# A two-layer hybrid trunk step on one core: mixing's multiply and subtract on VectorE, matmul filler held back for the attentions' ends, sink diagonals on ScalarE, first norm shared out

## The reference

```python
h = layer_norm(x) * (1 + scale) + shift            # adaLN from c (latent) or c_ctx (context)
p = h @ w_in                                        # 4096 columns: qa ka va ga qb kb vb gb uc vc gc
A: 8 q heads / 2 kv heads, d = 64, rms-normed q and k, axial rotary; full attention; context keys cached
B: same heads, windowed |i-j| <= 128, a learned sink logit per head in the softmax's denominator
C: per chunk of 128 positions and per group of 128 channels:
   y = u * (w_mix[g] @ v_n + b_mix[g])              # full 128x128 mixing over positions
each branch: o = out * silu(gate), y_r = o @ w_out_r
merge = sum over r of sigmoid(h @ w_gate_r) * y_r   # per-channel merge gates
x = layer_norm(ALPHA * x + gate_adaLN * (merge @ w_out), ln_g, ln_b)
```

## Time and profile before

| | |
|---|---|
| median of 3 runs | 1574.95 us (1574.42 to 1575.47) |
| the profiled execution's own time | 1575.67 us |
| its span | 1573.9 us |
| TensorE (matmul) busy | 1463.9 us, 93% |
| VectorE busy | 818.6 us, 52% |
| GpSimd busy | 796.3 us, 51% |
| ScalarE busy | 556.6 us, 35% |
| data moved | 126.90 MB, 81 GB/s over the span |

### The profile page before, as it was taken

The page is one execution under the profiler, slowest core; times in us unless marked ns, Lnnn a source line. Parts: engine busy times, 40 slices in busy tenths (PEclk is TensorE's granted clock), DMA queues, the critical chain, the costliest instruction groups (busy, mean ns, idle before and its releaser), DMA issues.

```text
span 1573.9 us, 21752 instructions
## 1 busy us (share of the span) xinstructions
PE 1463.9 (93%) x8776; PEld 1322.8 (84%) x8776; DVE 818.6 (52%) x1237; ACT 556.6 (35%) x843; POOL 796.3 (51%) x565
## 2 busy tenths in 40 slices
PE   4998998999998999899989999988999989998996
PEld 3798887889887888899868988887988879997985
DVE  4675677461788421111784757764448774011147
ACT  2333554333653211203233345542356422221130
POOL 1444676333666433724674547743246654464354
PEclk9999999999999999999999999999999999999999
DMA  7412000121100343344320220012111012214231
GB/s 301 144 54 71 27 28 14 67 71 67 41 28 27 117 151 123 132 147 146 122 86 35 85 67 28 27 41 71 54 54 41 27 47 101 81 68 166 89 107 67
DMA packets 36612, 126.90 MB, mean 81 GB/s; under 512 B 5024, under 2 KB 5664, under 8 KB 36512
## 3 DMA queue, kind: packets, MB, share of 16 engines
q1 hardware_dynamic: 29808, 108.54, 19.9%
q10 hardware_dynamic: 6704, 16.97, 2.9%
HBM read 119.73 MB, written 5.77 MB: 80 GB/s over the span
## 4 chain that ended last, share of the span: by engine, by line
PE 79%; DVE 9%; POOL 6%; issue 2%; ACT 2%; DVEq 0%; POOLq 0%; ACTq 0%
PE ps L899 43%; PE ps L847 6%; PE ps L849 6%; PE ps L848 6%; PE ps L1031 2%; PE ps L1029 2%; PE ps L1081 2%; PE ps L1058 2%; PE ps L1078 2%; POOL w_lo L1725 2%; PE ps L1057 2%; DVE o_inv L1610 2%; PE ps L1079 2%; PE ps L916 1%; POOL o_lo L1770 1%
## 5 line engine op out<-in xcount | busy, mean ns | idle before, releaser
L1725 POOL TENSOR_TENSOR w_lo<-raw,w_hi 128x1024 fp32r<-128x1024 f32 x148 | 359.2, 2434 | 345.0 <-ACT w_hi L1124 344.7
L899 PE MATMUL ps<-h_hi,w_hi 128*128 128x320 f32 x1280 | 300.0, 316 | 12.8 <-DVE g_c L1622 6.4
L899 PE MATMUL ps<-h_lo,w_hi 128*128 128x320 f32 x1280 | 293.6, 311 | 0.0
L899 PE MATMUL ps<-h_hi,w_lo 128*128 128x320 f32 x1280 | 293.3, 310 | 0.0
L1753 POOL TENSOR_TENSOR p_lo<-p_f,p_hi 128x512 fp32r<-128x512 f32 x164 | 212.7, 1301 | 155.1 <-ACT p_hi L1267 154.9
L899 PEld LDWEIGHTS ps<-h_hi,w_hi 128*128 128x128 f32 x1280 | 218.7, 190 | 34.0 <-DVE g_c L1622 8.1
L899 PEld LDWEIGHTS ps<-h_lo,w_hi 128*128 128x128 f32 x1280 | 217.1, 190 | 2.4
L899 PEld LDWEIGHTS ps<-h_hi,w_lo 128*128 128x128 f32 x1280 | 216.2, 189 | 2.4
L1124 ACT ACTIVATE w_hi<-raw 128x1024 fp32r<-128x1024 f32 x148 | 152.8, 1050 | 85.4 <-DMA raw<-in_weights 42.0
L1637 DVE TENSOR_TENSOR gy<-ps,sg 128x640 f32<-128x640 f32 x32 | 26.4, 824 | 255.5 <-PE ps L899 255.4
L1558 DVE TENSOR_REDUCE top<-ps 128x1 f32<-128x512 f32 (+1 forms) x128 | 83.5, 656 | 125.9 <-PE ps L1036 86.9
(11 more groups left out here) (177 smaller groups left out, 2640.4 us busy)
## 6 DMA issues: line engine op xcount, KB each, us to landing
raw<-in_weights SPq DMA_DIRECT2D x190, 512.0 KB, 3.3
raw_more<-in_weights SPq DMA_DIRECT2D x10, 512.0 KB, 10.7
x<-in_x_sample ACTq DMA_DIRECT2D x6, 512.0 KB, 8.0
x_mid<-x ACTq DMA_DIRECT2D x5, 512.0 KB, 2.6
x<-x_mid ACTq DMA_DIRECT2D x5, 512.0 KB, 6.7
y_sample<-x SPq DMA_DIRECT2D x4, 512.0 KB, 2.6
pack<-in_pack ACTq DMA_DIRECT2D x2, 528.0 KB, 4.6
x<-in_x_sample SPq DMA_DIRECT2D x2, 512.0 KB, 4.9
```

The source lines that it names most:

```text
L899: last = pe.matmul(ps[:, s + half, 0:HALF], w[:, u % RING, cols], acts[:, k, half * HALF:(half + 1) * HALF], start=k == 0 and part == 0, s ...
L1725: did(pool.tensor_tensor(w_lo[:, n % RING, :], raw_tile(r), w_hi[:, n % RING, :], ALU.subtract), w_ready)
```

## The change

It has six parts.

1. Mixing's multiply and subtract go from GpSimd to VectorE, directly behind the add, and signal a semaphore of their own, `mixed`, on which the y of branch 2 waits. The order is now mix 0, mix 1, z 0, mix 2, mix 3, z 1, instead of mix 0, z 0, mix 1, mix 2, z 1, mix 3.
2. `attention` takes `last_filler`, which it puts ahead of the product of the last group's first step: the last 5 of 48 chunks in A, the last 3 of 48 in B. The others are spread as before.
3. The event `dg` is gone; ScalarE makes the four diagonals itself, in its rounding step of the SINK slot.
4. xn of tiles 0 to 2 is made by ScalarE (scale and bias from GpSimd's `nmr`), of tiles 3 and 4 by VectorE. The `mod_row` copies of the first layer go from VectorE to ScalarE. The second pair's mod events stand ahead of h. TensorE waits once for all five xn.
5. `ones` moves from ahead of the first query tiles to behind kv tile 2, and kv tiles 0 and 1 stand ahead of gate 2 of A.
6. The last tile's second half is added on VectorE; its last pass goes in two halves of 512 columns, each stored by a DMA of its own.

The diff, cut to its core:

```diff
@@ -144,8 +145,6 @@
 for n, (g, i) in enumerate(steps):
-    if group_slots(br, g)[i] == SINK:
-        out.append(("dg", l, br, g))
     out.append(("ST", l, br, g, i))
@@ -154,6 +153,8 @@
 tick()
+if n == first[count - 1]:
+    out.extend(last_filler)
 product(n)
@@ -177,13 +178,16 @@
 def mods(p):
-    pair = (p, KT_D // 2 + p)
-    out.extend(("mod", 0, b, half) for b in pair for half in range(2))
-    out.extend(("col", 0, b) for b in pair)
+    out.extend(("mod", 0, b, half) for b in (p, KT_D // 2 + p) for half in range(2))
+def cols(p):
+    out.extend(("col", 0, b) for b in (p, KT_D // 2 + p))
 mods(0)
+cols(0)
 out.append(("split", 0))
 out.extend(("ht", 0, j) for j in range(KT_D))
+mods(1)
 for p in range(KT_D // 2):
@@ -191,7 +195,9 @@
 if p + 1 < KT_D // 2:
-    mods(p + 1)
+    if p:
+        mods(p + 1)
+    cols(p + 1)
 out.append(("mm", 0, "q_a", p))
@@ -233,8 +239,6 @@
     out.append(("table", l))
-if l == 0:
-    out.append(("ones", l))
@@ -252,8 +256,8 @@
 out.extend([qs[1], qs[2], *whole(gate("a", 0)), queries[1], qs[3], *whole(gate("a", 1)), queries[2], qs[4],
-            kvm[0], queries[3], qs[0], kvm[1], queries[4], *whole(gate("a", 2)), queries[0], *kv[0:3],
-            *whole(gate("a", 3)), keys[0], kv[3], keys[1], kv[4], keys[2], *whole(("z", l, 0, 0)), keys[3], keys[5],
+            kvm[0], queries[3], qs[0], kvm[1], queries[4], kv[0], kv[1], *whole(gate("a", 2)), queries[0], kv[2],
+            ("ones", l), *whole(gate("a", 3)), keys[0], kv[3], keys[1], kv[4], keys[2], *whole(("z", l, 0, 0)), keys[3], keys[5],
             keys[4], *whole(("z", l, 0, 1))])
@@ -267,7 +271,7 @@
     filler[-1] = (filler[-1], ("z", l, 0, j))
-out.extend(flat(attention(l, "a", filler, 3, 2, 4)))
+out.extend(flat(attention(l, "a", filler[:-5], filler[-5:], 3, 2, 4)))
 out.append(("pool", 0, 1, 2, 3, 4, 5, 6, 7))
@@ -291,7 +295,7 @@
         filler[-1] = (filler[-1], gate(br, c))
-out.extend(flat(attention(l, "b", filler, 3, 2, 4)))
+out.extend(flat(attention(l, "b", filler[:-3], filler[-3:], 3, 2, 4)))
 out.append(("pool", 0, 1, 2, 3, 4, 5, 6, 7))
@@ -307,8 +311,8 @@
 if begun:
-    out.extend([("mix", l, 0), *whole(("z", l, r, 0)), ("mix", l, 1), ("mix", l, 2), *whole(("z", l, r, 1)),
-                ("mix", l, 3)])
+    out.extend([("mix", l, 0), ("mix", l, 1), *whole(("z", l, r, 0)), ("mix", l, 2), ("mix", l, 3),
+                *whole(("z", l, r, 1))])
 else:
@@ -828,10 +832,17 @@
 for t in range(T):
-    sp.wait_ge(x_done, T * last + t + 1)
+    if t < T - 1:
+        sp.wait_ge(x_done, T * last + t + 1)
     dst = outs["y_prompt"][0] if t == 0 else outs["y_sample"][0, (t - 1) * P:t * P, :]
-    sp.dma_start(dst, x[:, t, :]).then_inc(final, 16)
-sp.wait_ge(final, 16 * T)
+    if t < T - 1:
+        sp.dma_start(dst, x[:, t, :]).then_inc(final, 16)
+    else:
+        for half in range(2):
+            sp.wait_ge(x_done, T * last + t + 1 + half)
+            cols = slice(half * BW, (half + 1) * BW)
+            sp.dma_start(dst[:, cols], x[:, t, cols]).then_inc(final, 16)
+sp.wait_ge(final, 16 * (T + 1))
@@ -974,8 +985,8 @@
 for t in range(T):
-    if j == 0:
-        pe.wait_ge(xn_ready, T * l + t + 1)
+    if j == 0 and t == 0:
+        pe.wait_ge(xn_ready, T)
     last = pe.transpose(slot(s)[:, t * P:(t + 1) * P], xn[:, t, j * P:(j + 1) * P], ident)
@@ -983,7 +994,10 @@
 if stage[0] == "y" and i == 0 and stage[3] == 0:
-    pe.wait_ge(o_done, O_PER_LAYER * l + (10, 20, 24)[stage[2]])
+    if stage[2] == 2:
+        pe.wait_ge(mixed, KT_B * (l + 1))
+    else:
+        pe.wait_ge(o_done, O_PER_LAYER * l + (10, 20)[stage[2]])
 channel_rows(stage, i, n)
@@ -1164,6 +1178,18 @@
     load(pack_loaded, pack[:, :], a["pack"][l])
+elif kind == "ln" and e[1] == 0:
+    for i, t in enumerate(XN_ON_ACT):
+        act.wait_ge(nmr_ready, i + 1)
+        did(act.activation(xn[:, t, :], x[:, t, :], ACT.Identity, bias=nmr[:, t:t + 1], scale=rstd[:, t:t + 1]),
+            xn_ready)
+elif kind == "mod" and e[1] == 0 and e[2] in FIRST_MODS:
+    if e[3]:
+        s = wait_filled(act, e[:3])
+        n = MODS.index(e[:3])
+        if n >= 2:
+            wait_filled(act, MOD_USER[n - 2])
+        did(act.activation(mod_row[:, n % 2, :], ps[:, s, 0:COLS], ACT.Copy), drained[s])
 elif kind == "h":
@@ -1259,7 +1285,12 @@
 if group_slots(br, g)[i] == SINK:
-    act.wait_ge(dg_made, NO[("dg",) + e[1:4]] + 1)
+    c = NO[("es",) + e[1:4]]
+    act.wait_ge(es_made, c + 1)
+    for h in range(GRP):
+        last = act.activation(p_f[:, n % 3, h * P:(h + 1) * P], ident, ACT.Copy, scale=es_f[:, c % 3, h:h + 1])
+        did(last, dg_made if h == GRP - 1 else None)
+    act.wait_ge(dg_made, c + 1)
 else:
@@ -1435,7 +1466,7 @@
 await_rstd()
-for t in range(T):
+for t in [t for t in range(T) if t not in XN_ON_ACT]:
     did(dve.tensor_scalar(xn[:, t, :], x[:, t, :], mv[:, t, 0:1], rstd[:, t:t + 1],
@@ -1454,7 +1485,7 @@
 elif kind == "mod":
-    if e[3] == 0:
+    if e[3] == 0 or e[1] == 0 and e[2] in FIRST_MODS:
         continue
@@ -1584,14 +1615,6 @@
                                  ALU.mult, ALU.mult), drained[s])
-elif kind == "dg":
-    step = ("ST",) + e[1:] + (len(group_slots(*e[2:])) - 1,)
-    n, c = NO[step], NO[("es",) + e[1:]] % 3
-    dve.wait_ge(es_made, NO[("es",) + e[1:]] + 1)
-    dve.wait_ge(p_lo_made, n - 2)
-    for h in range(GRP):
-        last = dve.tensor_scalar(p_f[:, n % 3, h * P:(h + 1) * P], ident, es_f[:, c, h:h + 1], None, ALU.mult)
-        did(last, dg_made if h == GRP - 1 else None)
 elif kind == "O":
@@ -1641,10 +1664,15 @@
     if n >= 2:
-        dve.wait_ge(o_done, O_DONE[MIXES[n - 2]])
+        dve.wait_ge(mixed, n - 1)
     did(dve.tensor_tensor(c_out[:, g % 2, :].rearrange("p (t n) -> p t n", t=T),
                           slot(s)[:, 0:TOK].rearrange("p (t n) -> p t n", t=T),
                           b_sp[:, g:g + 1, :].to_broadcast([P, T, P]), ALU.add), drained[s])
+    wait_drained(dve, ("gT", l, "u", g))
+    wait_drained(dve, e)
+    did(dve.tensor_tensor(c_out[:, g % 2, :], c_out[:, g % 2, :], g_c[:, g, :], ALU.mult), gated)
+    dve.wait_ge(o_hi_made, O_MADE[e])
+    did(dve.tensor_tensor(o_lo[:, g, :], c_out[:, g % 2, :], o_hi[:, g, :], ALU.subtract), mixed)
 elif kind == "m":
@@ -1662,6 +1690,10 @@
     drained[s])
+if (l, half, t) == (DEPTH - 1, 1, T - 1):
+    wait_drained(dve, e)
+    dve.wait_ge(x_alpha, T * l + t + 1)
+    half_summed[t] = did(dve.tensor_tensor(x[:, t, cols], x[:, t, cols], scaled[:, t % 2, :], ALU.add))
 if half == 0:
@@ -1669,7 +1701,8 @@
 after(half_summed[t])
-dve.wait_ge(x_summed, T * l + t + 1)
+if (l, t) != (DEPTH - 1, T - 1):
+    dve.wait_ge(x_summed, T * l + t + 1)
 ask_rstd(moments(t, [x[:, t, 0:512], x[:, t, 512:D]]))
@@ -1679,8 +1712,9 @@
     dve.wait_ge(ln_b_loaded, 16 * (l + 1))
-    did(dve.scalar_tensor_tensor(x[:, t, :], x[:, t, :], rstd[:, t:t + 1], ln_b_bc[:, :],
-                                 ALU.mult, ALU.add), x_done)
+    for cols in ((slice(0, BW), slice(BW, D)) if (l, t) == (DEPTH - 1, T - 1) else (slice(0, D),)):
+        did(dve.scalar_tensor_tensor(x[:, t, cols], x[:, t, cols], rstd[:, t:t + 1], ln_b_bc[:, cols],
+                                     ALU.mult, ALU.add), x_done)
 elif kind == "xt":
@@ -1732,12 +1771,12 @@
     root(rstd[:, t:t + 1], mv[:, t, 1:2], EPS, t)
-    pool.wait_ge(rstd_ready, asked[0])
-    pool.wait_ge(*did(pool.tensor_tensor(nmr[:, t:t + 1], mv[:, t, 0:1], rstd[:, t:t + 1], ALU.mult)))
-    did(pool.tensor_scalar(nmr[:, t:t + 1], nmr[:, t:t + 1], -1.0, None, ALU.mult), nmr_ready)
+    shift(t)
 elif kind == "ln" and e[1] == 0:
     for t in ARRIVAL:
         root(rstd[:, t:t + 1], mv[:, t, 1:2], EPS, t)
+        if t in XN_ON_ACT:
+            shift(t)
 elif kind in ("ln", "vn"):
@@ -1760,14 +1799,8 @@
     n = NO[e]
-    pool.wait_ge(o_hi_made, O_DONE[e])
+    pool.wait_ge(o_hi_made, O_MADE[e])
     did(pool.tensor_tensor(og_part(o_lo, g), og_sum(n), og_part(o_hi, g), ALU.subtract), o_done)
-elif kind == "mix":
-    _, l, g = e
-    wait_drained(pool, e)
-    did(pool.tensor_tensor(c_out[:, g % 2, :], c_out[:, g % 2, :], g_c[:, g, :], ALU.mult), gated)
-    pool.wait_ge(o_hi_made, O_DONE[e])
-    did(pool.tensor_tensor(o_lo[:, g, :], c_out[:, g % 2, :], o_hi[:, g, :], ALU.subtract), o_done)
 elif kind == "y" and e[2] >= 1:
@@ -1777,7 +1810,7 @@
     did(pool.tensor_tensor(kept_lo[n][:, :], raw_tile(r), kept_hi[n][:, :], ALU.subtract), kept)
-elif kind == "out" and e[2] == 1:
+elif kind == "out" and e[2] == 1 and e[1:] != (DEPTH - 1, 1, T - 1):
     _, l, _, t = e
```

27 lines of the change are left out of this document (16 added, 11 removed).

## The result

The changed kernel takes **1520.29 us** (median of 4 runs, 1520.01 to 1520.94) against 1574.68 of the kernel before in 4 runs (1573.22 to 1575.47). The ratio is 0.9657, 95% interval 0.964 to 0.9673: 54.4 us faster. The prediction said 1517, between 1504 and 1541. The profiled execution took 1520.94 us, its span is 1519.1, 54.8 shorter than before.

A forecast was written before the change was run, and what follows sets the result against it. TensorE was taken as the bound, busy 1463.9 of 1573.9 us, leaving only its idle time and lower-clock time to win. Terms summed to -58.5 from 1575.67, giving 1517 us, range 1504 to 1541.

The forecast's parts named there:

- One hold per layer: Mixing: a VectorE SBUF instruction waits beside a GpSimd w_lo pass, 2.1 us more; 1.5 us given back over both layers.
- the rival in which GpSimd holds VectorE through the stage: Mixing: its waits stay, +15 to 1532 us; chance 0.22, shared with the other 1532 case.
- 2.0 for the body: Attention bodies, thinner filler: one new wait of 1.0 us in each of four bodies, +4.0 us in all.
- The clock term: Behind the o_sum wait at attention A's end: slower clock loses 2.5 us per layer, counted as saved with the wait.
- 2.5 was taken: Attention B, diagonals on ScalarE: its own half of the g_c evictions gets later, 2.5 us given back.
- the 5.3: First norm: with three xn tiles and the mod_row copy on ScalarE, VectorE is through 5.3 us earlier, at about 19.8.
- The signs it named: Profile after, several stages: what waits, clock, VectorE times, ScalarE load and transposes' start should show if the forecast holds.
- the prediction's bound of 50 us: TensorE's list of waits: the forecast is wrong if they still add up to more than 50 us.
- ScalarE late in attention B: Rival, attention B: ScalarE's diagonals delay TensorE at each of 20 sink steps, 64 us, 1581 us; chance 0.05.
- The rival of the end chain that moves with the filler: Attentions' ends: o_sum moves back with TensorE, 27 us lost, 1544 us; chance 0.08, shared with both 1532 cases together.
- With nothing held up anywhere: Rival, whole kernel: no new waits anywhere, -75.9 us to 1500; chance 0.15 for 1500 to 1508.

The follow-up runs named there:

- The six-chunk run: The changed kernel with the last 6 chunks of attention B's filler held back for its end instead of 3; 1506.85 us.
- the best kernel here: The changed kernel with 6 chunks of attention B's filler held back and xn of tiles 0 to 3 on ScalarE; 1505.21 us.

## Why the prediction was right, and where it wasn't

**The total** is right by 3 us, and the signs of all six parts are. One size isn't, that of attention B with the diagonals, which came 8 us short. That the total is so close is in part luck: 3.7 us came in stretches that the sum didn't count and 1.1 more at mixing than was forecast.

**Part 1** (-15.0): 16.1 in the timeline. One hold per layer, as taken; the rival in which GpSimd holds VectorE through the stage stays away because GpSimd, now free, goes through both w_lo passes at once and is idle behind them (5.78 us ahead of 638.23), so only one of the four SBUF instructions of the last two groups meets it.
The Trainium skill, "GPSIMD Engine Reference", section 1, names VectorE instructions with two SBUF inputs as those that contend with GpSimd. The trace agrees with it on the multiply (2.07 and 2.33 instead of 0.82). The scaling of xn has one tensor input and is held just the same (3.56 us for two tiles, 0.81 for one alone). The section's other case, a two-port performance mode, would cover it. The rows fit that: a scaling takes 0.54 us for 512 elements and 0.81 for 1024, 0.5 ns for each more, while the multiply or subtract of two tensors takes 0.69 for 512 and 0.82 for 640, 1.0 ns for each more. No run here switches the mode off, so it isn't shown as the cause.

**Part 2, A** (-12.0 and 2.0 for the body): 9.7 in the timeline, 8.4 by undoing it. The waits were right to the hundredth, and the body cost 0 instead of 2. The clock term, 2.5 us in each layer, has to be looked for outside of the 9.7, because most of it lay behind the attention's end, in the kv_b stretch. Before, the five us behind this wait are at 0.50 in both layers (267.30 and 1034.80), now they are at 1.00. TensorE's idle time in the kv_b stretch is 5.26 us in both layers of both kernels, and its busy time fell by 0.1 us in layer 0 and by 3.0 in layer 1: this is where the row of 0.1 + 3.0 comes from. In layer 0 the gain was lost again behind the later wait of 2.99 us, where the clock was 1.00 before and is 0.66 now; in layer 1 it was 0.50 there and is 0.66. So the term was right where it was read, and wrong was to take the clock behind a wait as a loss that nothing else changes.

**Part 2, B, and part 3** (-15.0 and -5.5, 2.0 for the body; 18.5 in all): 7.9 us inside the attention, 10.7 with the v_c stage behind it, and 10.5 by undoing both. This is the step that was wrong, though the total held. The prediction had "one new wait of 1.0 us" for the thinner body; the profile has 4.12 and 3.48, and 4.0 more for ScalarE's g_c where 2.5 was taken. The rows for it were there before: the earlier trace rows list g_c with 6.4 us in 4, and the prediction took that for VectorE's load alone, which part 3 would relieve; it rose to 8.0. It is also the place of the chunk behind a gate's boundary, which needs the only pair of banks. The six-chunk run shows it: the same work on every engine, the chunks placed otherwise, and 13.4 us come out; of the waits that went, half were on VectorE's evictions and half on ScalarE's. And the two parts were added where they share a limit: undone singly they cost 1.4 and 2.6, together 10.5.

**Part 4** (-6.5): 6.4. The terms inside were off and cancelled: the transposes came 3.7 earlier (21.63 from 25.35) and not 5.3, because of the hold beside w_lo. (The prediction's words give the 5.3 to VectorE; by its own rows VectorE would be through at 19.8 instead of 17.51 + 5.73 = 23.24, 3.4 earlier, and 5.3 is what the transposes' start at "near 20" would gain.) Between them and the first q_a matmul another 2.7 came, where the second mod_row wait (3.1) went and a wait of 1.4 for h_lo took its place. Of the 6.4, 5.5 are idle time and 1.0 clock, which the sum hadn't counted there.

**Part 5** (-8.0): 7.3 in the timeline, 6.1 by undoing it. **Part 6** (-0.5): 0.8; the affine pass of the last tile but one is at 1.28 us from the 2.16 of the earlier trace rows.

**The signs it named.** No wait on mixing's low half, no o_sum wait, a clock of 1.00 behind both attentions and 82 us of ScalarE came as said; the transposes begin at 21.6 instead of near 20, and 1.9 us of k_st wait stayed. The seven lines of the earlier trace rows make up 55.8 us and not 53.8, and 11.7 now; the prediction's bound of 50 us can only be meant for them, since the whole list of waits is at 61.5.

**The rivals.** ScalarE late in attention B: it is busy 81.97 of 130.8 us there, the 82 that were worked out, and it cost waits of 4 us in all, not 64. The rival of the end chain that moves with the filler is refuted for A, and near the truth for B as long as the diagonals are on ScalarE, where 2.6 us is left of what the three chunks were to bring; with the diagonals on VectorE it is 9.1. With nothing held up anywhere the prediction had 1500; the best kernel here reaches 1505.

**Left open.** What decides whether a wait of a given length is followed by lost clock isn't shown, so the parts' clock losses can't be told from each other to better than 1 to 2 us. How much of the 13.4 us of the six-chunk run belongs to the moved chunk and how much to the new spacing wasn't separated. The memsets themselves weren't made smaller, and filler with a second pair of banks in B wasn't tried.

## What to carry to other kernels

Independent work that fills a wait has to be checked for what it waits for itself: with one buffer, the place of the piece that crosses from one output to the next counts, and here 3 or 6 pieces held back differ by 13 us. Two edits that relieve the same chain shouldn't be added up; undo both and each, and look for the limit that they share. And a move to a faster engine pays only with the cover behind it, as at mixing: undoing the order alone cost 7.5 us and undoing the engine alone 12.7, of some 16 for both.

## What wasn't expected of the hardware

The clock behind a wait isn't a fixed price. Waits of the same length in the same place of the program, in two kernels and two layers (windows of before, then of the changed kernel, each right behind such a wait; columns as in rows 3):

```profile
328.50:333.50 5.00, 4.52 (x30) 4.28 (x31) 3.24 (x2) 0.76 (x2) 1.87 (x1) 1.00 0.31 105
1096.20:1101.20 5.00, 5.00 (x19) 5.00 (x20) 2.41 (x1) 0.00 (x0) 1.86 (x1) 0.50 0.31 105
```

```profile
308.50:313.50 5.00, 5.00 (x24) 5.00 (x25) 2.41 (x1) 0.00 (x0) 1.87 (x1) 0.66 0.29 105
1058.10:1063.10 5.00, 5.00 (x24) 5.00 (x25) 2.44 (x1) 0.00 (x0) 1.89 (x1) 0.66 0.33 105
478.10:482.10 4.00, 4.00 (x13) 3.63 (x14) 0.00 (x0) 0.00 (x0) 2.34 (x2) 0.50 0.15 33
1228.60:1232.60 4.00, 3.97 (x23) 3.73 (x24) 1.59 (x1) 1.51 (x3) 3.27 (x4) 1.00 0.02 4
```

The first four stand behind a wait of 2.99 us: the granted clock is 1.00, 0.50, 0.66 and 0.66, so between nothing and 2.5 us is lost. The last two stand behind the bank wait, 4.12 us with half the clock (1.2 GHz) and 3.48 with all of it (2.4 GHz). Nor is it fixed by the place: with nothing held back in attention A, the waits of 4.24 and 4.23 us at its end are followed by 0.66 and 0.52, and the same 2.99 us waits behind them by 1.00 in both layers, where the changed kernel has 0.66. A sum that prices waits with their clock should carry it as a range, from zero to half of the window, and expect part of what it saves at one wait to be lost at the next.
